# Output projections of a hybrid decoder step: the first two tiles computed together, reload, weight split and high parts issued earlier

## The reference

```python
def rmsnorm(x, g):
    x32 = x.astype(jnp.float32)
    y = x32 * lax.rsqrt(jnp.mean(x32 * x32, axis=-1, keepdims=True) + EPS)
    return (y * g.astype(jnp.float32)).astype(x.dtype)
...
for l in range(DEPTH):
    h = rmsnorm(x, norm_g[l, 0])
    if l % 2 == 0:
        # mLSTM heads (512 features) and forgetting attention (512 features)
        mixed = jnp.concatenate([hm, hf], axis=-1)
        out = mixed @ w_out                 # 1024 x 1024, "out0"
    else:
        # RWKV-7 time mixing
        out = y.astype(h.dtype) @ w_o       # 1024 x 1024, "out1"
    x = x + rmsnorm(out, norm_g[l, 1])
    h = rmsnorm(x, norm_g[l, 2])
    x = x + rmsnorm(swiglu(h, ffn_w_gate[l], ffn_w_up[l], ffn_w_down[l]), norm_g[l, 3])
```

## Time and profile before

| | |
|---|---|
| median of 3 runs | 3203.37 us (3196.29 to 3209.23) |
| the profiled execution | 3191.59 us, span 3189.9 us |
| TensorE busy | 2993.4 us (94%) |
| TensorE weight loads | 2809.9 us (88%) |
| VectorE, ScalarE, GpSimd busy | 1576.0, 957.1, 1333.1 us (49%, 30%, 42%) |
| TensorE's mean granted clock | 0.975 of full speed |
| first projection, out0 | its first product starts at 572.25 us of the span |
| second projection, out1 | its first product starts at 2324.47 us of the span |

### The profile page before, as it was taken

The page is one execution under the profiler, slowest core; times in us unless marked ns, Lnnn a source line. Parts: engine busy times, 40 slices in busy tenths (PEclk is TensorE's granted clock), DMA queues, the critical chain, the costliest instruction groups (busy, mean ns, idle before and its releaser), DMA issues.

```text
span 3189.9 us, 73305 instructions
## 1 busy us (share of the span) xinstructions
PE 2993.4 (94%) x32208; PEld 2809.9 (88%) x32208; DVE 1576.0 (49%) x2110; ACT 957.1 (30%) x1641; POOL 1333.1 (42%) x1016
## 2 busy tenths in 40 slices
PE   7999988999999999979999889999889999999996
PEld 6989855879999999969999877787787999999996
DVE  4232265248666631254222156798524866663125
ACT  5132265232111111133211256676523211111112
POOL 2322310326777743421423322343232677774321
PEclk9999999999999999999999889999999999999998
DMA  3443454222223234212422313322142222323411
GB/s 109 124 130 109 147 174 139 77 90 80 80 81 110 77 128 143 52 71 100 153 86 93 102 47 99 77 70 59 57 161 89 80 80 82 110 77 127 143 39 62
DMA packets 342471, 312.25 MB, mean 98 GB/s; under 512 B 35335, under 2 KB 303059, under 8 KB 341020
## 3 DMA queue, kind: packets, MB, share of 16 engines
q1 hardware_dynamic: 325706, 275.99, 28.6%
q10 hardware_dynamic: 16466, 31.83, 2.7%
HBM read 212.79 MB, written 94.62 MB: 96 GB/s over the span
## 4 chain that ended last, share of the span: by engine, by line
PE 45%; DVE 4%; issue 2%; ACT 1%; DMA 1%; SPq 0%; POOL 0%; DVEq 0%; ACTq 0%; POOLq 0%
PE PS L519 18%; PE PS L686 12%; PE PS L2841 2%; PE PS L2853 1%; PE PS L2847 1%; PE PS L2835 1%; PE PS L2831 1%; PE PS L2961 1%; PE PS L700 1%; DVE act_lo L2558 1%; PE PS L2827 1%; PE PS L2886 1%; PE PS L2432 1%; PE PS L3022 0%; PE PS L2918 0%
## 5 line engine op out<-in xcount | busy, mean ns | idle before, releaser
L519 PE MATMUL PS<-act_hi,w_hi 128*128 128x344 f32 x1968 | 631.9, 321 | 25.8 <-DVE act_lo L2192 12.1
L519 PE MATMUL PS<-act_lo,w_hi 128*128 128x344 f32 x1968 | 629.0, 320 | 0.0
L519 PE MATMUL PS<-act_hi,w_lo 128*128 128x344 f32 x1968 | 628.5, 319 | 0.0
L500 POOL CAST w_hi<-w_raw 128x1024 fp32r<-128x1024 f32 (+1 forms) x118 | 128.1, 1086 | 1037.7 <-issue 456.2
L519 PEld LDWEIGHTS PS<-act_hi,w_hi 128*128 128x128 f32 x1968 | 370.9, 188 | 30.0 <-issue 20.1
L519 PEld LDWEIGHTS PS<-act_hi,w_lo 128*128 128x128 f32 x1968 | 370.9, 188 | 0.0
L519 PEld LDWEIGHTS PS<-act_lo,w_hi 128*128 128x128 f32 x1968 | 370.9, 188 | 0.0
L686 PE MATMUL PS<-T,wq_S 128*128 128x258 f32 x2880 | 365.7, 283 | 0.0
L686 PE MATMUL PS<-act_hi,wq_A 128*128 128x258 f32 x1920 | 364.4, 282 | 0.0
L686 PEld LDWEIGHTS PS<-T,wq_S 128*128 128x128 f32 x2880 | 354.4, 189 | 0.0
L686 PEld LDWEIGHTS PS<-act_hi,wq_A 128*128 128x128 f32 x1920 | 305.4, 190 | 0.0
(11 more groups left out here) (620 smaller groups left out, 5928.3 us busy)
## 6 DMA issues: line engine op xcount, KB each, us to landing
hidd<-hid_out SPq DMA_DIRECT2D x44, 516.0 KB, 3.4
w_raw<-in_ffn_w_gate_dram SPq DMA_DIRECT2D x44, 512.0 KB, 4.8
w_raw<-in_ffn_w_up_dram SPq DMA_DIRECT2D x44, 512.0 KB, 6.1
w_raw<-in_ffn_w_down_dram SPq DMA_DIRECT2D x32, 512.0 KB, 3.9
hid_in<-hidd SPq DMA_DIRECT2D x28, 516.0 KB, 7.4
proj<-stage ACTq DMA_DIRECT2D x24, 516.0 KB, 2.7
xT<-xkeep SPq DMA_DIRECT2D x3, 4128.0 KB, 18.0
rw<-z_st SPq DMA_DIRECT2D x24, 516.0 KB, 2.7
```

Of the source, the lines that this page charges most:

```text
L500: nc.gpsimd.tensor_copy(w_hi[:, u, 0:kts, :], w_raw[:, u, 0:kts, :]).then_inc(w_hi_done, 1)
L519: mm = nc.tensor.matmul(PS[:, 3 * u + c, 0:CH], w[:, u, kt, :], x[:, kt, CH * c:CH * c + CH], start=(kt == 0 and part == 0), stop=(kt == k ...
```

## The change

1. A new function `pair_tensor` computes output tiles 0 and 1 of both projections: tile 0 with feature tiles 0 to 3, tile 1 with 0 to 3, then both with feature tiles 4 to 7, one feature tile at a time. Its products are written out, not looped. `gemm_tensor` then does the other three pairs. The number of products is the same.
2. out0: in the last step of attention ScalarE makes the four early high parts before the copies of `R7` and `DG1`, VectorE makes the first low part before it scales the last block, and GpSimd's wait before the weight split is for `DV1` on TensorE (the samples' last product with the cached values, right ahead of `PV31`) instead of `DG1` on ScalarE.
3. out1: SyncE issues the store of item 14 and the early reload of the 1024 prompt columns ahead of the eight stores of `e_yt`, and the 8 sample columns of the same feature tiles in two more transfers after these have landed. `mix_loaded` has the counts that go with it.
4. out1: the wait for the stores of the prompt state (`SC["s_out"]`) moves from ahead of `mix_sync` to behind it, ahead of the reload of `xT`.

```diff
+        def pair_tensor(pe, name, r):
+
+            k = plan[name]
+            for kts, us in ((range(HK), (0,)), (range(HK), (1,)), (range(HK, KT), (0, 1))):
+                for kt in kts:
+                    for u in us:
+                        if kt == 0:
+                            pe.wait_ge(w_split[u], k[u] + 1 + START)
+                            pe.wait_ge(psum_free[u], k[u] + START)
+                        pe.wait_ge(act_ready, KT * r + kt + 1 + START)
+                        for c in range(NCH):
+                            for part, (w, x) in enumerate(((w_hi, act_hi), (w_hi, act_lo), (w_lo, act_hi))):
+                                mm = nc.tensor.matmul(PS[:, 3 * u + c, 0:CH], w[:, u, kt, :], x[:, kt, CH * c:CH * c + CH],
+                                                      start=(kt == 0 and part == 0), stop=(kt == KT - 1 and part == 2))
+                        if kt == KT - 1:
+                            mm.then_inc(psum_full[u], 1)
...
-            mix_early(sp, 0, mix)
+            mix_early(sp, 0, mix, slice(0, T))
...
+                if j == FSTEPS:
+                    mix_split_scalar(act, 1, 0, range(EARLY))
                 if j and j % 4 == 0:
...
+                if j == FSTEPS:
+                    dve.wait_ge(FT.sem, FT[f"PV{j - 1}"] + START)
+                    mix_split_vector(dve, 1, 0, range(1))
                 if j and j % 4 == 0:
...
-        def mix_split_scalar(act, r, n):
-            for k in range(KT):
-                act.wait_ge(mix_in[k // 2], 16 * n + 16 + START)
+        def mix_loaded(eng, n, k):
+            eng.wait_ge(mix_in[k // 2], (16 if n == 0 else 48 if k < EARLY else 32) + START)
+
+        def mix_split_scalar(act, r, n, ks):
+            for k in ks:
+                mix_loaded(act, n, k)
...
                 if k == ITEMS - 1:
                     out_weights(sp, "out1", kt_of("rwkv_w_o"), range(1))
+                if k == ITEMS:
+                    sp.wait_ge(out_st[0], 16 * (ITEMS // 2) + START)
+                    sp.wait_ge(BP.sem, BP.of("pY", ITEMS - 1))
+                    mix_early(sp, 1, mix2, slice(0, TP))
                     sp.wait_ge(QV.sem, QV["yt"] + START)
                     rows = mix2[:, TP:T].rearrange("(kb k4 e dh r) b -> kb e dh r k4 b", kb=2, k4=4, e=2, dh=2)
...
-                if k == ITEMS:
-                    sp.wait_ge(out_st[0], 16 * (ITEMS // 2) + START)
                     sp.wait_ge(e_out, 16 * 12 + START)
-                    sp.wait_ge(BP.sem, BP.of("pY", ITEMS - 1))
-                    mix_early(sp, 1, mix2)
+                    mix_early(sp, 1, mix2, slice(TP, T))
...
-            sp.wait_ge(SC["s_out"], 16 * NG + START)
             sp.wait_ge(out_st[1], 16 * (ITEMS // 2) + START)
...
             mix_sync(sp, 1, mix2, range(EARLY // 2, 4))
+            sp.wait_ge(SC["s_out"], 16 * NG + START)
             sp.dma_start(xT[:, :, :].rearrange("p k t -> p (k t)"), xkeep[:, :]).then_inc(x_back, 16)
...
-            pool.wait_ge(FA.sem, FA["DG1"] + START)
+            pool.wait_ge(FT.sem, FT["DV1"] + START)
             split_pairs(pool, "out0", 4, KT)
...
-            gemm_tensor(pe, "out0", 4, 1)
+            pair_tensor(pe, "out0", 1)
+            gemm_tensor(pe, "out0", 3, 1, 1)
...
-            gemm_tensor(pe, "out1", 4, 7)
+            pair_tensor(pe, "out1", 7)
+            gemm_tensor(pe, "out1", 3, 7, 1)
```

More of the change, by code:

```diff
@@ L2184, in mix_split_scalar, with mix_split_vector @@
                 nc.scalar.copy(act_hi[:, k, :], mixed(n, k)).then_inc(hi_ready, 1)
-        def mix_split_vector(dve, r, n):
-            for k in range(KT):
-                dve.wait_ge(mix_in[k // 2], 16 * n + 16 + START)
+        def mix_split_vector(dve, r, n, ks):
+            for k in ks:
+                mix_loaded(dve, n, k)
                 dve.wait_ge(hi_ready, KT * r + k + 1 + START)
@@ L3532, in _ @@
             scan_scalar(act)
-            mix_split_scalar(act, 7, 1)
+            mix_split_scalar(act, 7, 1, range(KT))
             keep_scalar(act, "out1", 5, 7)
@@ L3547, in _ @@
             fox_vector(dve)
-            mix_split_vector(dve, 1, 0)
+            mix_split_vector(dve, 1, 0, range(1, KT))
             stats_vector(dve, 1)
@@ L3556, in _ @@
             scan_vector(dve)
-            mix_split_vector(dve, 7, 1)
+            mix_split_vector(dve, 7, 1, range(KT))
             stats_vector(dve, 5)
```

6 lines of the change are left out of this document (3 added, 3 removed).

## The result

| | before | changed |
|---|---|---|
| median of 21 runs each, side by side | 3201.87 us | 3210.57 us |
| ratio, 95% interval | | 1.0032 (1.0023 to 1.0042) |
| span of the profiled execution | 3189.9 us | 3203.6 us |

The account below looks back on a forecast made before the run. It took TensorE, busy for 94% of the span, as the bound, so only idle or cold-clock time could be won. Out0 -1.3 and out1 +5.8 gave +4.5 us on a median of 3203.4: 3208 us, range 3196 to 3217.

Parts of the forecast that it names:

- Both projections, the uncovered split: After each pair, GpSimd's 4.0 us split for tile 2 has only 1.4 us of cover: TensorE idle 2.6 us, twice.
- Out0, start: out0: TensorE starts at 568.7 instead of 572.25, 3.5 us earlier (2.7 to 4.5); tile 2 then starts 1.3 us earlier.
- Out1, store, reload and `e_yt`: out1: item 14's store lands at 2314.7, `e_yt` at 2323.2; TensorE starts at 2328.2 instead of 2324.47.
- The rival that `e_yt` passes the reload: out1: `e_yt` stores are down at 2321.5, tile 2 +4.1 us; sum +2.8, 3206 us; chance 0.2.
- the one that item 14's store passes the loads: out1: item 14's store lands ahead of the weight loads; out1 at 0, sum -1.3, 3202.1 us; chance 0.08.
- Out1, to tile 2: out1: tile 2 starts at 2357.0 instead of 2351.2, +5.8 us (0 to +7.5), after its weights at 2353.1 and their split.
- The clock rival: New TensorE gaps in both projections: clock falls, 2.5 us once or twice; sum +7 to +9.6, 3212 us; chance 0.22.

Follow-up runs that it names:

- out1 only: The changed kernel with `gemm_tensor` and the old waits back at out0, all else as changed; ratio to the kernel before 1.0026 (1.0014 to 1.0037).
- tile by tile: The changed kernel with the pair's last four feature tiles taken for tile 0, then for tile 1; ratio to the kernel before 1.0007 (0.9996 to 1.0019).
- best version: Kernel before plus out0 changes, pairs' second halves tile by tile, item 15 before tile 0's split, out1 weights of tiles 2 and 3 before `xT`'s reload; ratio 0.9980.
- pair order only: The kernel before with `pair_tensor` in both projections and nothing moved; ratio to the kernel before 1.0029 (1.0016 to 1.0041).
- the change again: The same changed kernel, run and profiled again in another session; ratio to the kernel before 1.0038 (1.0026 to 1.0051).
- change with item 15 first: The changed kernel with item 15 made on GpSimd ahead of out1's split of tile 0's weights; ratio to the kernel before 1.0036 (1.0025 to 1.0048).
- out0-only: The changed kernel with out1 and SyncE's queue put back as before; ratio to the kernel before 0.9995 (0.9984 to 1.0007).
- no pair order: The changed kernel with both projections tile by tile through `gemm_tensor`, all moved steps kept; ratio to the kernel before 1.0021 (1.0011 to 1.0031).

## Why the prediction came out right, and where it was too low

The verdict and the mechanism were as forecast; the size was not: +4.5 us against a measured +10 (7 to 13). The 3208 us of the forecast look closer to the 3210.6 us than they are, since the kernel before had a median of 3201.9 us in this comparison and not 3203.4. (The upper end of the range isn't what its words add up to: 3203.4 + 9.6 + 7 is 3220, not 3217.) By its steps, with out1's times on the clock of before:

- **Both projections, the uncovered split: right, a little small.** 2.6 us forecast (at out1 the numbers of the forecast make it 3.5, because it has tile 2's weights come last), 2.88 to 2.93 us in all twelve gaps of seven profiles. The split took what it took before (tile 0's copy starts at 597.01 and the split ends at 598.20 + 2.78 = 600.98, 4.0 us as in the earlier trace rows); the forecast had left out the quarter of a microsecond from there to the first product at 601.23.
- **Out0, start: right in its cause, late by 0.3 us.** The first product waits for `fx_o` behind the early low part, which took 2.96 us (2.6 taken); 5.69 us after `PV31`, with 5.4 forecast. The wait of 1.63 us for the third low part was in no step, and it cost little: in this profile the first products were already at the high clock (0.42 us and none slow), while in the other kernels with this start 9 to 11 of them were slow and the wait there was 0.3 us or none; both come to the third feature tile at 4.7 us. Tile 2 starts 0.3 us earlier instead of 1.3. On the clock of before it starts at 596.65 us instead of the forecast 595.8, and the old tile 2 started at 596.93 us, not at 597.1.
- **Out1, store, reload and `e_yt`: right in the profile of the change.** Store landed 2314.1 us (2314.7 forecast), `e_yt` down 2323.2 (2323.2), first product 2328.1 (2328.2), item 15 ready 2330.5 (2329.3), `mix_sync` 2332.9 (2332.3). The rival that `e_yt` passes the reload and the one that item 14's store passes the loads both fell: that store took 2.53 us to issue, and 3.3 to 3.7 us in other executions, behind loads that had taken 15.43. The five other profiles with this order have the early reload at 7.3 to 9.1 us after item 14 instead of 6.53, and the first product at 21.4 to 23.1 us instead of 20.58, so the first profile is the mildest here. (The forecast's 3.5 us for issuing the `e_yt` stores leaves out the one of 2.47 us that it names; they took 4.19.)
- **Out1, to tile 2: mis-sized.** Forecast: 23.9 us from the first product to tile 0's end, from the 8.5 us of the earlier trace rows. Measured: 26.1. VectorE's second low part waited for GpSimd's item 15, as the rows below show. On TensorE this is a break of 0.85 us and a slow restart, 1.2 us together. And the clock stayed low for 8.2 us after the first product instead of 5.3: 25 slow products instead of 19, each 0.13 us longer, another 0.8 us. So tile 2 is 7.3 us late instead of 5.8. This stretch took 25.3 to 26.1 us in the three executions with the pair order at out1 and item 15 late, and 23.4 to 23.8 us in the three where item 15 was early. The weights of tile 2, which the forecast named as what holds it, landed at 2353.4 us (issued at 2341.85, 19.1 us to landing; 2353.1 forecast), but tile 0 ended at 2354.2 instead of 2352.1 and came last, by 0.8 us.
- **The clock rival, given 0.22: mostly true.** Of the twelve gaps of 2.88 to 2.93 us, ten were followed by a tile of 12.9 to 14.3 us at the low clock instead of one of 11.55, 1.3 to 2.8 us each. The two exceptions are those of the change's first profile. Price and place were right (2.5 us, once or twice), the chance was not: the earlier trace rows showed one idle of 2.46 us that kept the clock, and I read it as a reason against, although the new gaps are longer. The one row was no measure of the chance: the same idle ahead of L407 is in all twelve profiles, and in three of them (out1 only, tile by tile, best version) the clock was at 0.50 from 1.5 us behind it.

VectorE's low parts of out1, in the changed kernel:

```profile
2333.80 1.70 DVE L2217 TENSOR_TENSOR act_lo<-early_in,act_hi 128x1032 fp32r<-128x1032 f32 x1 [13.10 <-ACT act_hi L2209]
2338.12 3.52 DVE L2217 TENSOR_TENSOR act_lo<-early_in,act_hi 128x1032 fp32r<-128x1032 f32 x3 [2.63 <-POOL q_o L2840]
```

The second part has its inputs at about 2335.5 us, but starts when item 15's last operation (2336.71 + 1.28) ends. The program has no semaphore between the two. The Trainium skill ("SBUF — State Buffer", SBUF: two separate sides) has the two engines share one port pair under an exclusive lock: whichever starts first keeps it for the whole instruction, and the other stands still. By that rule item 15, made late, can delay the low parts; the rows agree. They show one thing more: VectorE also went without between item 15's two operations, 0.08 us apart. Before, item 15 was over at 2322.9 us, 1.6 us ahead of TensorE's start. The break of 0.84 to 0.86 us is in all five executions in which item 15 comes after TensorE's first product, and in none of the others.

The sum in the terms of the first profile: out0 -0.2, out1 +7.3. In the others the clock adds 1.3 to 2.8 us at out0 and 1.5 to 1.6 at out1, which gives 10 to 11.5 us, and out1 starts 0.8 to 2.5 us later than in the first profile. The runs without a profile speak for the clock too. The profiled execution had a mean granted clock of 0.975, the highest of the 21 runs of the change, whose mean is 0.972. Beside the kernel before on the same chip, the mean of the runs is lower by 0.0011 to 0.0018 in the four other comparisons with the largest loss (out1 only, pair order only, the change again, change with item 15 first). Of 3200 us, 0.0013 is some 8 us more at half speed and so, behind dense products, about 4 us of time (an estimate). The out0-only kernel has +2.5 us in its profile but -5 to +2 in its runs, and the mean clock of these is 0.0009 above that of the kernel before, so the low clock of its profile isn't typical of it. In which gap each run lost the clock isn't shown. What made the first profile's two gaps differ from the ten others isn't known either: the idle time is the same to 0.05 us, and what TensorE did ahead of them is too.

## What to carry to other kernels

- Two tiles that end together put the refill of the first one's buffers on the path. Interleave what is wanted late (the first halves), and let the tiles end apart by at least the refill: here 5.6 us against 4, worth 3.4 us at out0, where the pair order gave only 0.2.
- An earlier start counts only if the next thing on the path is early too: at out0, 2.2 of 2.9 us went into waiting for the last four feature tiles, and the low clock behind that wait took 1.7 more, until the order wanted them later. A large reload ahead of small stores for which a split, two more reloads and an item of work wait loses more than it gives; put the small ones first.
- A new gap of 2 to 3 us on TensorE can cost more than its length, because the clock may fall in it, and one profile may miss this. Take a second profile of the same kernel, and compare the granted clock of all runs.

## What the runs showed of the hardware

- A short gap behind dense products is followed by the low clock in some executions and not in others, and by these counts more often the longer it is. Gaps of 2.88 to 2.93 us were followed by the low clock in ten of twelve cases. The gap of 2.46 us ahead of L407, the same in all twelve profiles, was followed by it in three. One of 2.19 us was (no pair order, out0); one of 1.99 us (the same kernel, out1) and one of 1.31 us were not. From the first product of out1 it took 2.4 to 9.1 us until the products were fast again: 5.3 before, 8.2 and 2.4 in the two profiles of the change, 9.1 with the second half tile by tile. The break of 0.85 us is in both extremes, so it isn't what decides.
- A small store that is issued while a reload of 2 MB is in flight lands late: item 15's store held the next transfer for 7.4 us in the best version, where such stores had landed in 2.4 to 3.5 us, and the eight `e_yt` stores 8.2 us from the first issue. The Trainium skill ("DMA: Bandwidth & Descriptors", Queues, rings and completion order) has an engine take the descriptors of a ring in their order; these landings agree with it.
- The twelve executions, of eleven kernels that are alike up to there in all that `PV31` waits for, differ by up to 11 us in its time, of which this case shows no cause. A stage has to be compared from its own start: in three kernels with an unchanged out0 it ended 101.53 to 101.54 us after `PV31`.
